# Samples' projections with the samples stationary in four column groups, and another order on VectorE and ScalarE at the phase boundary

## The reference, cut to what matters

```python
p = xs @ kv_w + kv_b            # k, v, logf   (shared_kv)
p = h @ w_in + b_in             # q, z of the attention layer, h = x*(1+scale)+shift
logits = q k^T / 8 + c_q - c_k  # causal, softmax in fp32
y = (softmax(logits) @ v * silu(z)) @ w_out + b_out
```

## Time and profile before

| | |
|---|---|
| median of three runs | 1894.65 us |
| the profiled execution | 1887.75 us, span 1886.2 us |
| mean granted TensorE clock | 0.958 of 2.4 GHz |
| PE busy | 1737.4 us, 92% |
| weight loads (PEld) | 1507.9 us, 80% |
| VectorE (DVE) | 963.9 us, 51% |
| ScalarE (ACT) | 637.2 us, 34% |
| GpSimd (POOL) | 405.8 us, 22% |
| chain that ended last | PE 72%, DVE 11%, issue 5%, ACT 5%, DMA 4%, POOL 2% |
| sample projections (L1796) on that chain | 2% |

### The profile page before, as it was taken

One profiled execution on the slowest core, in us unless ns is written; L12 is line 12 of the kernel. 1 busy time (PEld: TensorE's weight loads), 2 busy tenths in 40 slices (PEclk: granted clock), 3 DMA queues, 4 the chain that ended last, 5 costly groups with the idle time before them and its releaser, 6 DMA issues.

```text
span 1886.2 us, 28075 instructions
## 1 busy us (share of the span) xinstructions
PE 1737.4 (92%) x10256; PEld 1507.9 (80%) x10256; DVE 963.9 (51%) x1459; ACT 637.2 (34%) x987; POOL 405.8 (22%) x424
## 2 busy tenths in 40 slices
PE   5999999999999969998699999999999999769866
PEld 2999989999999969998577878877777877547632
DVE  6423354343343362255524656555656465689763
ACT  5312222112121262244232645544454546252120
POOL 0000011111111000012212333424251524254130
PEclk8999999999999999999799999999999999589978
DMA  8111122122221213243222121121112031428493
GB/s 327 45 44 44 33 90 79 67 89 89 78 78 67 89 48 104 90 146 107 72 90 76 46 68 45 67 67 56 56 56 78 33 87 39 121 80 297 164 376 137
DMA packets 50190, 180.43 MB, mean 96 GB/s; under 512 B 6522, under 2 KB 8186, under 8 KB 48850
## 3 DMA queue, kind: packets, MB, share of 16 engines
q1 hardware_dynamic: 32802, 120.30, 18.8%
q0 software_dynamic: 17328, 59.33, 8.9%
HBM read 154.07 MB, written 17.15 MB: 91 GB/s over the span
## 4 chain that ended last, share of the span: by engine, by line
PE 72%; DVE 11%; issue 5%; ACT 5%; DMA 4%; POOL 2%; SPq 0%; POOLq 0%; DVEq 0%; ACTq 0%
PE bank L1629 18%; PE bank L1631 17%; PE bank L1630 17%; PE bank L1796 2%; PE bank L1866 2%; DMA pages<-cache_v 2%; PE bank L1917 2%; DMA bs_b<-bs_row 2%; PE bank L1733 2%; PE bank L1896 2%; POOL p_lo L529 1%; PE bank L1897 1%; PE bank L1918 1%; PE bank L1919 1%; DVE pages L1353 1%
## 5 line engine op out<-in xcount | busy, mean ns | idle before, releaser
L1629 PE MATMUL bank<-h_hi,w_lo 128*128 128x344 f32 x1152 | 373.0, 324 | 1.2 <-DVE w_lo L1009 1.2
L1630 PE MATMUL bank<-h_lo,w_hi 128*128 128x344 f32 x1152 | 367.5, 319 | 0.0
L1631 PE MATMUL bank<-h_hi,w_hi 128*128 128x344 f32 x1152 | 367.2, 319 | 0.0
L529 POOL TENSOR_TENSOR p_lo<-parg,p_hi 128x512 fp32r<-128x512 f32 (+1 forms) x192 | 203.7, 1075 | 212.8 <-ACT p_hi L899 211.0
L1629 PE MATMUL bank<-x_hi,w_lo 128*128 128x512 f32 x528 | 223.8, 424 | 7.7 <-POOL x_lo L486 6.4
L1629 PEld LDWEIGHTS bank<-h_hi,w_lo 128*128 128x128 f32 x1152 | 216.6, 188 | 5.0 <-issue 5.0
L1630 PEld LDWEIGHTS bank<-h_lo,w_hi 128*128 128x128 f32 x1152 | 216.5, 188 | 0.5 <-issue 0.5
L1631 PEld LDWEIGHTS bank<-h_hi,w_hi 128*128 128x128 f32 x1152 | 216.4, 188 | 0.0
L1630 PE MATMUL bank<-x_lo,w_hi 128*128 128x512 f32 x528 | 211.3, 400 | 0.0
L1631 PE MATMUL bank<-x_hi,w_hi 128*128 128x512 f32 x528 | 211.1, 400 | 0.0
L1629 PE MATMUL bank<-y_hi,w_lo 128*128 128x320 f32 (+2 forms) x512 | 177.3, 346 | 26.7 <-ACT y_hi L720 9.6
(11 more groups left out here) (300 smaller groups left out, 2816.7 us busy)
## 6 DMA issues: line engine op xcount, KB each, us to landing
raw<-units SPq DMA_DIRECT2D x121, 512.0 KB, 3.3
ada_ring<-w_ada SPq DMA_DIRECT2D x32, 512.0 KB, 3.3
pages<-cache_k POOLq DMA_DIRECT2D x32, 512.0 KB, 5.4
pages<-cache_v POOLq DMA_DIRECT2D x32, 512.0 KB, 16.4
ada_first<-w_ada SPq DMA_DIRECT2D x8, 1024.0 KB, 11.8
ckb<-scr_c POOLq DMA_DIRECT2D x16, 512.0 KB, 4.5
KX<-KA SPq DMA_DIRECT2D x32, 256.0 KB, 4.3
scr_x<-x1f POOLq DMA_DIRECT2D x8, 512.0 KB, 3.8
```

Source lines behind the costliest of these rows:

```text
L529: g.tensor_tensor(p_lo[:, r, off:HALF], parg[:, r, off:HALF], p_hi[:, r, off:HALF].bitcast(F32), ALU.subtract).then_inc(S("p_ready"), 1)
L1629: mm(out, lhs_lo, rhs_hi, start=first, stop=False)
L1630: mm(out, lhs_hi, rhs_lo, start=False, stop=False)
L1631: return mm(out, lhs_hi, rhs_hi, start=False, stop=last)
```

## The change

In the eight phases the samples become the stationary side. `sample_rows` (in place of `sample_cols` there; the forget logits keep `sample_cols`) loads nine columns of activations and moves 128 weight columns, block k in the column group k % 4, so that each group sums two blocks, and the result stands in rows 32g to 32g+8 of `bank(q % 2)[:, 0:128]`. VectorE copies these 128 x 128 numbers to `samp` (`take_samples`), PE adds and turns them with one matmul against `fold4` into `bank(q % 2)[:, 128:137]`, at step n = 5, 3, 2 or 2 of the unit (`FOLD_AT`), and `evac_s` takes them from there.

VectorE's order in a phase: `take_samples` stands where `evac_s` stood or at the very beginning, and `evac_s` one or two instructions later. At the beginning of a phase come `take_samples(j+1, 0)`, `v_lo(j)` and `gate_o(j-1, 1)`; the last two stood at the end of the phase before, in the other order. On ScalarE `kq_high(j+1, 0)` goes ahead of `probs(j, 11)`.

`mask8` loses its constant place to `samp` and is made later by GpSimd, after the last phase's projections, in memory that is free by then. The constants' semaphores are merged into one (`pc`).

```diff
@@ -180,6 +180,7 @@
         qtok = at("qtok", [NS, D], F32, R3 + 20480)
+        mask8 = at("mask8", [NS, NS, H], F32, R2 + 65536)
         omask = at("omask", [P, D], F32, R3 + 20480)
@@ -229,7 +230,8 @@
         fS = const("fS", [H, NS])
-        mask8 = const("mask8", [NS, NS, H])
+        samp = const("samp", [P, P])
+        fold4 = const("fold4", [P, 9])
         maskp = const("maskp", [P, NS])
@@ -237,7 +239,6 @@
         dn = const("dn", [P, 4])
-        fold4 = const("fold4", [P, 9])
         oS = at("oS", [P, KB, NS], F32, R3 + 12032)
@@ -270,6 +271,7 @@
         KIND = (0, 2, 1, 3)
+        FOLD_AT = (5, 3, 2, 2)
@@ -440,23 +442,20 @@
             g.memset(identb[:, :], 1.0).then_inc(S("pc"), 1)
-            g.memset(mask8[:, :, :], 1.0).then_inc(S("pc"), 1)
             g.memset(maskp[:, :], 1.0).then_inc(S("pc"), 1)
-            pool.wait_ge(S("pc"), 6)
+            pool.wait_ge(S("pc"), 5)
             for m in (ident, identb):
                 g.affine_select(out=m[:, :], in_=m[:, :], compare_op=ALU.is_equal, fill=0.0, base=0,
-                                pattern=[[-1, P]], channel_multiplier=1).then_inc(S("consts"), 1)
+                                pattern=[[-1, P]], channel_multiplier=1).then_inc(S("pc"), 1)
...
             g.affine_select(out=maskb[:, :], in_=maskb[:, :], compare_op=ALU.is_gt, fill=0.0, base=0,
-                            pattern=[[1, P]], channel_multiplier=-1).then_inc(S("consts"), 1)
-
-            g.affine_select(out=mask8[:, :, :], in_=mask8[:, :, :], compare_op=ALU.is_equal, fill=0.0, base=0,
-                            pattern=[[1, NS], [0, H]], channel_multiplier=-1).then_inc(S("consts"), 1)
+                            pattern=[[1, P]], channel_multiplier=-1).then_inc(S("pc"), 1)
+
             g.affine_select(out=maskp[:, :], in_=maskp[:, :], compare_op=ALU.is_ge, fill=0.0, base=0,
                             pattern=[[-H, NS]], channel_multiplier=1).then_inc(S("pc"), 1)
-            pool.wait_ge(S("pc"), 7)
+            pool.wait_ge(S("pc"), 9)
             g.affine_select(out=maskp[:, :], in_=maskp[:, :], compare_op=ALU.is_ge, fill=0.0, base=H - 1,
-                            pattern=[[H, NS]], channel_multiplier=-1).then_inc(S("consts"), 1)
+                            pattern=[[H, NS]], channel_multiplier=-1).then_inc(S("pc"), 1)
@@ -565,6 +564,10 @@
             pool.wait_ge(S("mm"), 12 * KB)
+            g.memset(mask8[:, :, :], 1.0).then_inc(S("pc"), 1)
+            pool.wait_ge(S("pc"), 11)
+            g.affine_select(out=mask8[:, :, :], in_=mask8[:, :, :], compare_op=ALU.is_equal, fill=0.0, base=0,
+                            pattern=[[1, NS], [0, H]], channel_multiplier=-1).then_inc(S("pc"), 1)
@@ -950,9 +953,10 @@
                     z_tanh(j + 1, 0)
+                if more:
+                    kq_high(j + 1, 0)
                 probs(j, 11)
                 if more:
-                    kq_high(j + 1, 0)
                     z_tanh(j + 1, 1)
@@ -1023,7 +1027,7 @@
             v.tensor_tensor(sc2[:, :, 9:18], scT[:, :, :], sc2[:, :, 0:9].bitcast(F32), ALU.subtract).then_inc(S("sc_ready"), 1)
-            dve.wait_ge(S("consts"), 5)
+            dve.wait_ge(S("pc"), 10)
             v.tensor_tensor(fold[:, :], ident[0:18, 0:9], ident[0:18, 9:18], ALU.add).then_inc(S("sc_ready"), 1)
@@ -1289,11 +1293,17 @@
+            def take_samples(j, q):
+
+                dve.wait_ge(S("mm"), 12 * j + 3 * q + 1)
+                settle(dve, S("settled"))
+                v.tensor_copy(samp[:, :], bank(q % 2)[:, 0:P]).then_inc(S("samp_ready"), 1)
+
             def evac_s(j, q):
...
                 kind = KIND[q]
-                dve.wait_ge(S("mm"), 12 * j + 3 * q + 1)
-                v.tensor_scalar(kqvzS[:, kind, j, :], bank(q % 2)[:, 0:9], col_at("b_kqvz", kind * KB + j), None, ALU.add)\
+                dve.wait_ge(S("samp_fold"), 4 * j + q + 1)
+                v.tensor_scalar(kqvzS[:, kind, j, :], bank(q % 2)[:, P:P + 9], col_at("b_kqvz", kind * KB + j), None, ALU.add)\
                     .then_inc(S("ev_s"), 1)
@@ -1418,13 +1428,17 @@
             split_lo(0, 1)
+            take_samples(0, 0)
             evac_s(0, 0)
...
             link(v.tensor_copy(ccol[:, :, :], bank(6)[:, 0:TT * H].rearrange("p (t h) -> p h t", h=H)))
+            take_samples(0, 1)
             evac_s(0, 1)
             split_lo(0, 2)
+            take_samples(0, 2)
             evac_s(0, 2)
             split_lo(0, 3)
+            take_samples(0, 3)
             evac_s(0, 3)
@@ -1435,12 +1449,17 @@
                 later = not isinstance(j, int) or j > 0
+                if more:
+                    take_samples(j + 1, 0)
+                if later:
+                    v_lo(j)
+                    gate_o(j - 1, 1)
                 key_decay(j)
+                if not more:
+                    tok(1, qtok1, 0)
+                peak(j, 0)
                 if more:
                     evac_s(j + 1, 0)
-                else:
-                    tok(1, qtok1, 0)
-                peak(j, 0)
                 peak(j, 1)
@@ -1451,9 +1470,11 @@
                 if more:
-                    evac_s(j + 1, 1)
+                    take_samples(j + 1, 1)
                 peak(j, 5)
                 peak(j, 6)
+                if more:
+                    evac_s(j + 1, 1)
                 peak(j, 7)
@@ -1462,12 +1483,14 @@
                 if more:
-                    evac_s(j + 1, 2)
+                    take_samples(j + 1, 2)
                 else:
...
                 exponents(j, 3)
+                if more:
+                    evac_s(j + 1, 2)
                 if later:
@@ -1483,11 +1506,12 @@
                 if more:
-                    evac_s(j + 1, 3)
+                    take_samples(j + 1, 3)
                 else:
...
                 if more:
+                    evac_s(j + 1, 3)
                     split_lo(j + 2, 0)
@@ -1504,14 +1528,12 @@
                     kq_low(j + 1, 1)
-                gate_o(j, 1)
-                if more:
-                    v_lo(j + 1)
...
             phase(KB - 1, False)
+            gate_o(KB - 1, 1)
             invert(KB - 1, 1, 0)
@@ -1529,6 +1551,7 @@
                 link(v.tensor_copy(sn[:, 1, :], bank(6)[0:NS, 0:H]))
+                dve.wait_ge(S("pc"), 12)
                 for c in range(2):
@@ -1796,6 +1819,13 @@
+            def sample_rows(out, slot, src):
+
+                for k in range(KB):
+                    rows = slice(32 * (k % 4), 32 * (k % 4) + 9)
+                    last = mm(out[rows, :], src[:, k, :], raw[:, slot, k, :], start=k < 4, stop=k >= 4)
+                return last
+
             def token_step(out, slot, half, k):
@@ -1829,9 +1859,12 @@
                     pe.wait_ge(S("lo_ready"), U_B + 4 * j + q + 1)
-                    last = sample_cols(bank(q % 2)[:, 0:9], slot, hS if q >= 2 else x1S)
+                    last = sample_rows(bank(q % 2)[:, 0:P], slot, hS if q >= 2 else x1S)
                     last.then_inc(S("mm"), 1)
                     wait(pe, *((S("zs_done"), 4 * j - 1) if q == 0 else (S("ev_h"), 6 * j + 2 * q)))
+                if n == FOLD_AT[q]:
+                    pe.wait_ge(S("samp_ready"), 4 * j + q + 1)
+                    mm(bank(q % 2)[:, P:P + 9], samp[:, :], fold4[:, :], start=True, stop=True).then_inc(S("samp_fold"), 1)
                 if n == KB:
```

## The result

Four runs of the changed kernel took 1858.57 to 1869.84 us, median 1862.07; the kernel before has a median of 1894.18 over four. The ratio is 0.9848, 95% interval 0.9814 to 0.9882, so the change takes off 1.5%. A second timing beside other kernels gave 0.9846 (0.9826 to 0.9867). The forecast was 1869 within 1854 to 1884, and its sum was -20.9 us. The profiled execution took 1859.98 us (span 1858.5), 27.8 less than the one before; the two medians differ by 32.1.

The account below looks back on a forecast made before the run. PE, busy in 92% of the span, was taken as the bound. Terms -17.0 +3.2 -4.9 -6.7 +6.0 -2.9 -2.4 +0.5 +3.0 +0.3 = -20.9 took 1887.75 to 1866.8; forecast 1869 us, range 1854 to 1884.

Parts of the forecast that it names:

- Part 1: Samples on PE: a call falls from 1.70 to 0.58 us, a fold of 0.31 is added, net 0.81 saved.
- Part 2: VectorE's 32 copies out of PSUM, 0.29 us each, 9.3 together, cost nothing while PE's fold comes later.
- Part 3: At q=1, 2, 3, 21 calls give -17.0 us; PE waits for kf at q=1, 0.46 us seven times, +3.2.
- Part 4: Boundary into phases 1 to 6: calls -4.9 us, Vst wait -6.7, p_lo(11) delayed by KA's low half +6.0.
- Part 5: Last boundary, to j=7: QA 1.5 us sooner, Vst 1.4 more, -2.9 us; mask8 costs nothing.
- Part 6: Ahead of the loop: q=1 to 3 -2.4 us, +0.5 back; q=0's fold +3.0; call for j=1 +0.3.
- Nothing bites: GpSimd wins both times, kf is in time, the prelude costs 0: -33 us, 1855; chance 0.15.
- Evacuation becomes the wait: Copy or column 0.4 us late at three places per phase, slow prelude clock: 12 us back, 1879; chance 0.21.
- No overlap: The sample column groups do not overlap, 32 x 0.31 us are added: about +9, 1897; chance 0.06.
- GpSimd starved: At the boundary p_lo(11) is held out until QA's low half ends: +30 us, 1897; chance 0.05.
- The forecast case: Whole kernel: the main forecast, 1860 to 1878 us, chance 0.53.

Follow-up runs that it names:

- the one-group kernel: The changed kernel with all eight sample blocks in one column group, folded by a 9 x 9 identity: 1908.96 us, ratio 1.0071 to the kernel before.
- the split halves: ScalarE's kq_high(j+1,0) split around probs(j,11), on the changed kernel with first copy and split_lo(j+1,2) early, q=1 samples behind peak(j,5): 1847.38 us, ratio 0.9754.
- the kernel with only the two orders: The kernel before with only the change's VectorE and ScalarE orders, samples in columns, no copy, no fold: 1883.93 us, ratio 0.994.

## Why the prediction held, and where its sum was short

**Part 1** held in its net, and not term by term. The call is 0.56 us against 0.58, but 0.09 us stand ahead of it (scores, 1.01 instead of 0.93; transposes, 0.99 instead of 0.90), which I had not counted: 0.65. The fold is 0.23 against 0.31, since its load is hidden behind the token matmul before it. Net 1.70 - 0.65 - 0.23 = 0.82 a call, forecast 0.81: two errors, of 0.07 and 0.08, cancel, and that is luck. That the groups must overlap is shown by the one-group kernel.

**Part 2** held: the 32 copies take 9.2 us, VectorE has 7 us more work in all, and no copy holds PE in the loop.

**Part 3** held: PE waits for kf in seven phases, 0.40 us by the length of the samples' slot (0.96 instead of 0.56), forecast 0.46. It goes when the samples move behind peak 5, and when the call is long again (one column group).

**Part 4** had the mechanism, and a size was off. The Vst wait went, and gave 1.25 us or more a boundary instead of 1.1. The price on GpSimd came at the place named, but it is 0.60 us (values(11) takes 1.22 instead of 0.62) and not 1.0. GpSimd, boundary before phase 2, to be laid beside the 1.00 of the earlier trace rows:

```profile
1154.45 1.85 POOL L528 TENSOR_TENSOR p_lo<-parg,p_hi 128x128 fp32r<-128x128 f32 x2 [3.10 <-ACT p_hi L902]
```

The pair is stretched by 0.85 us and not by the 1.45 of my working. My end at 1159.95 amounts to both halves of p_lo, 1.0 us, behind the end of KA's low half at 1158.9. The pair ends only 0.3 us behind it (1156.30 against 1155.99), so GpSimd got in between. The term of the sum that was mis-sized most is this one: +6.0 forecast, +3.6 measured at the same six boundaries. It also stands at a seventh, into phase 7, which the sum left out: PE has 14 waits for p_lo, seven at values(0) and seven at values(11). That KA's low half is what stretches the pair is shown: with ScalarE's old order it takes 1.00 us again, with the split halves 1.30, and the wait goes both times.

**Part 5** held: QA's wait fell by 1.72 us and Vst's by 1.42, together 3.1 against 2.9. mask8 cost nothing seen on PE.

**Part 6** held in its place, and its size was short: the loss at the first fold was there, where PE waits 5.0 us. From the first samples to those of q=1 the kernel needs 3.9 us more (21.48 against 17.59), forecast +3.0; PE runs at 1.2 GHz for 3 us behind the wait. From call to call only this stretch and the one behind the call for j=1 (18.54 against 18.32 us, +0.3 forecast) became longer by the change.

**The sum.** A phase was to shrink by 2.9 us and shrinks by 3.60: 0.40 more from p_lo, 0.15 from Vst, 0.06 from the kf wait, 0.04 from the four calls, and 0.07 that are not placed, between the samples of q=2 and those of q=3. Over six phases that is 4.3 us, over half of the 7 by which the sum of -20.9 missed the 27.8 between the two profiled executions. The rest is nearly the clock and the start: the profile of before has a phase of 90.35 us (1247.33 to 1337.68) among others of 87.2, in which PE runs at 1.2 GHz for some 7 us; a second such stretch ahead of the loop (granted clock 0.51 from 947 to 950 us) costs it 1.5 us by the same stretch of the kernel with only the two orders, which has none there; and it reached the stage 2.2 us sooner. Together 2.5 us. The sum had no term for this.

The 1.2 GHz stretches may themselves belong to the samples in columns. First the kernel before, then the kernel with only the orders, then the changed one, with the granted clock third from the right:

```profile
1289.00:1295.00 6.00, 6.00 (x17) 5.14 (x17) 1.89 (x2) 0.20 (x1) 2.08 (x3) 0.50 0.26 87
```

```profile
1251.00:1254.00 3.00, 3.00 (x10) 2.52 (x11) 2.94 (x4) 2.84 (x4) 0.00 (x0) 0.52 1.03 246
1514.00:1517.00 3.00, 3.00 (x8) 2.32 (x8) 2.96 (x4) 2.32 (x4) 0.00 (x0) 0.50 0.99 258
```

```profile
995.00:1570.00 575.00, 565.56 (x3189) 444.79 (x3188) 352.85 (x621) 288.73 (x485) 229.85 (x215) 1.00 0.19 61
```

In the loop the profile of before has one such stretch, the one with only the orders has three, with 1.5 us lost at each of the three, and each begins during a call in columns or at once behind it (calls at 1286.99; 1249.59, 1375.90 and 1512.06). None of the ten profiles with samples in rows has one from 995 to 1560 us, the one-group kernel with its long calls included. That is a coincidence in few profiles, and no run tests it; but if it is no chance, the new form also gives back some 3 to 5 us that no part of the prediction counted.

**The rivals.** "Nothing bites" fell: three waits appeared, worth 3.9 + 2.8 + 4.2 us (p_lo's at seven boundaries). "Evacuation becomes the wait" holds at one place out of 32, the first fold; in the undone VectorE order it holds at six more. The Trainium skill's rule (TensorEngine Tiling (Array Packing), PSUM Bottleneck), that the copy out of PSUM may become the bottleneck after a fourfold speedup, agrees with these places only. At them the copy was late by its place in VectorE's order, not by VectorE's load, which is 52% of the span. "No overlap" and "GpSimd starved" did not happen. The forecast case was right in its mechanism; its time of 1869 lies 7 us above the median of 1862.07, about what the sum missed.

## What to carry to other kernels

A few vectors against a big matrix in fp32: put the vectors in the stationary side and spread the contraction over four column groups; here a call went from 1.70 us to 0.65 and a fold of 0.23, and without the groups nothing was gained. It buys a round trip over VectorE, so the copy must be first in VectorE's order at that point, and the fold as many steps later as the queue ahead of the copy needs: up to 1.7 us a boundary were lost in the loop where it was not, and 5.0 us once ahead of the loop. When the bound engine gets faster, look for the next release of each of its waits: three of them (kf, p_lo, the first fold) held back 11 us. Moves of a line or two gave back the first fold and kf, and 5 us of an older wait for p_lo at values(0); that the new one for p_lo came back shows in the trace alone.

## What the runs showed of the hardware that was not expected

- The samples' matmuls with nine stationary columns have 0.09 us ahead of them, in one column group as in four: the last token matmul starts 0.33 us before them in both kernels, and 0.23 before the samples in columns. And an fp32 fold over nine rows instead of 128 takes 0.31 us and not 0.14: its weight load starts at 1180.14 with the matmul, while the load of the full fold starts at 1161.65, 0.23 us before its matmul, beside the token matmul. Both go with a change of the shape of the stationary side; that this is the cause is argued, not tested.
- Where a VectorE instruction with two SBUF inputs overlaps GpSimd's subtraction, the delay falls mostly on GpSimd: four p_lo with one split beside them take 0.96 us more, the split 0.02 to 0.1 (1.24 and 1.32 us instead of 1.22); at the boundary p_lo takes 0.85 more and KA's low half 0.21 (2.68 instead of 2.47). That the two contend agrees with the Trainium skill's GPSIMD Engine Reference, Key points. Here the delay was removed by moving the one VectorE instruction into an idle 1.4 us.
